# A one-layer decoder step on eight cores: values before keys in the mixer, convolution and sample work between attention steps, gate before up, and a new order of the first loads

## The reference

```
def decoder_layer(x, p, s0, conv0, ng, ...):
    h = x + 0.5 * rms_norm(swiglu(rms_norm(x, ng[0]), f1_gate, f1_up, f1_down), ng[1])
    mix, s_new, conv_new = token_mixer(rms_norm(h, ng[2]), s0, conv0, ...)
    h = h + rms_norm(mix, ng[3])
    h = h + 0.5 * rms_norm(swiglu(rms_norm(h, ng[4]), f2_gate, f2_up, f2_down), ng[5])
    gate = jax.nn.sigmoid(rms_norm(h, ng[6]) @ w_ple_gate)
    h = h + rms_norm((p @ w_ple_proj) * gate, ng[7])
    return h, s_new, conv_new
...
def token_mixer(u, s0, conv0, ...):
    q, k, v, g, r, cb, cc, ch = jnp.split(u @ w_in, points, axis=-1)
    log_a = log_sigmoid(r @ w_gate_up + b_gate) / 16
    o, s_new = gla_chunked(q, k, v, log_a, s0)
    o = rms_norm(o, gla_norm_g) * silu(g)
    oc = cb * conv3(cc * ch)
    return concat([o, oc]) @ w_out, s_new, conv_new
```

## Time and profile before

| | |
|---|---|
| median of 3 runs | 1643.7 us (1640.93 to 1648.77) |
| profiled execution | 1645.65 us, span of its slowest core 1644.0 us |
| spans of the eight cores | 1631.0 to 1644.0 us, mean granted TensorE clock 0.967 to 0.975 |
| busy, share of the span | PE 93%, DVE 44%, ACT 45%, POOL 16% |
| DMA | 305.39 MB, mean 186 GB/s |

### The profile page before, as it was taken

One profiled execution on the slowest core, in us unless ns is written; L12 is line 12 of the kernel. 1 busy time (PEld: TensorE's weight loads), 2 busy tenths in 40 slices (PEclk: granted clock), 3 DMA queues, 4 the chain that ended last, 5 costly groups with the idle time before them and its releaser, 6 DMA issues.

```text
span 1644.0 us, 27962 instructions; the slowest of 8 cores (1631.0 to 1644.0 us)
## 1 busy us (share of the span) xinstructions
PE 1537.0 (93%) x9454; PEld 1492.4 (91%) x9454; DVE 715.9 (44%) x1421; ACT 736.5 (45%) x1437; POOL 268.5 (16%) x512
## 2 busy tenths in 40 slices
PE   6999999899998999999989999799998998999996
PEld 5999889889997999989989999799998997889995
DVE  3331464543324643155554422573315754433136
ACT  3112665642147611275574124841138474511266
POOL 3211210112121221111112112022111110111110
PEclk9999999999998999998999999899999995999998
DMA  9865843468666796565446668399556443566661
GB/s 282 255 186 160 233 142 102 112 181 250 186 193 191 208 328 209 170 184 167 102 156 208 200 176 249 112 279 319 177 160 202 137 142 100 158 177 175 203 190 69
DMA packets 83452, 305.39 MB, mean 186 GB/s; under 512 B 9538, under 2 KB 12498, under 8 KB 82548
## 3 DMA queue, kind: packets, MB, share of 16 engines
q0 software_dynamic: 73040, 283.97, 58.4%
q1 hardware_dynamic: 10276, 19.65, 3.7%
HBM read 292.83 MB, written 10.75 MB: 185 GB/s over the span
## 4 chain that ended last, share of the span: by engine, by line
PE 79%; DMA 7%; ACT 6%; DVE 4%; issue 4%; DVEq 0%; SPq 0%; ACTq 0%; POOLq 0%; POOL 0%
PE ps_bank L472 78%; DMA sb_wring<-f2a 3%; DMA sb_wring<-f2b 2%; ACT L519 2%; DMA sb_wring<-f1b 1%; ACT sb_xnB L519 1%; DVE sb_hB L522 1%; DVE sb_xnB L522 1%; DMA sb_ngl<-ngl 1%; ACT sb_ta L519 1%; PE ps_bank L496 1%; ACT sb_WA L519 1%; PE ps_bank L504 0%; ACT sb_sqB L519 0%; DVE sb_WA L527 0%
## 5 line engine op out<-in xcount | busy, mean ns | idle before, releaser
L472 PE MATMUL ps_bank<-sb_xnA,sb_wring 128*128 128x344 f32 x2208 | 410.6, 332 | 19.0 <-DVE sb_WA L527 8.6
L472 PE MATMUL ps_bank<-sb_xnB,sb_wring 128*128 128x344 f32 x2208 | 396.6, 323 | 6.6 <-ACT sb_xnB L519 5.7
L472 PEld LDWEIGHTS ps_bank<-sb_xnA,sb_wring 128*128 128x128 f32 x2208 | 370.1, 197 | 27.2 <-issue 26.0
L472 PEld LDWEIGHTS ps_bank<-sb_xnB,sb_wring 128*128 128x128 f32 x2208 | 358.2, 190 | 13.5 <-issue 13.1
L472 PE MATMUL ps_bank<-sb_WA,sb_wring 128*128 128x344 f32 x1872 | 330.7, 323 | 11.4 <-DVE sb_WA L527 4.7
L472 PE MATMUL ps_bank<-sb_WB,sb_wring 128*128 128x344 f32 (+1 forms) x1904 | 333.7, 320 | 1.7 <-DVE sb_wring L522 1.0
L472 PEld LDWEIGHTS ps_bank<-sb_WA,sb_wring 128*128 128x128 f32 x1872 | 301.6, 189 | 17.8 <-issue 17.5
L472 PEld LDWEIGHTS ps_bank<-sb_WB,sb_wring 128*128 128x128 f32 x1904 | 309.1, 190 | 2.6 <-issue 2.4
L607 POOL DMA_DIRECT2D sb_wring<-f2a x132 | 69.7, 528 | 367.1 <-PE ps_bank L472 334.9
L519 ACT ACT_TABLE_LOAD x91 | 116.8, 1283 | 27.4 <-DMA sb_ngl<-ngl 14.4
L607 POOL DMA_DIRECT2D sb_wring<-f1a x132 | 69.7, 535 | 290.7 <-PE ps_bank L472 280.7
(11 more groups left out here) (198 smaller groups left out, 1647.6 us busy)
## 6 DMA issues: line engine op xcount, KB each, us to landing
sb_wring<-f1a POOLq DMA_DIRECT2D x132, 512.0 KB, 10.0
sb_wring<-f2a POOLq DMA_DIRECT2D x132, 512.0 KB, 5.5
sb_wring<-f1b POOLq DMA_DIRECT2D x48, 704.0 KB, 5.5
sb_wring<-f2b POOLq DMA_DIRECT2D x48, 704.0 KB, 5.3
sb_wring<-wca POOLq DMA_DIRECT2D x24, 512.0 KB, 6.8
sb_wring<-wo POOLq DMA_DIRECT2D x24, 512.0 KB, 5.6
sb_wring<-wpg POOLq DMA_DIRECT2D x24, 512.0 KB, 7.3
sb_wring<-wg POOLq DMA_DIRECT2D x12, 512.0 KB, 6.7
```

The source lines that it names most:

```text
L472: ins = e.matmul(out.ap, a.ap, b.ap, start=(first and i == 0), stop=(last and i == n_ - 1))
```

## The change

1. **First loads.** After `ngl` and A's x are put among the pending operations, all pending ones are issued at once; B's x follows. In the planner's model a load by SP of over 400 columns now takes link time.
2. **Gate first.** In both feed-forwards the gate product and its weights go ahead of the up product, and the gate's VectorE and ScalarE operations are queued before the up product is asked for.
3. **Mixer.** Values ahead of keys and queries, right behind E and Einv; convolution chunk 1 is no longer ahead of the keys. In tiles 0 to 3 the three attention steps now hold chunks 1, 2 and 3; in tiles 4 and 5 chunks 1 to 3 run before the steps. The weights' order in the ring follows. `Einv` moves to W from 6n (the later place of convolution chunks 2 and 3), `sp` to `S.sq`.
4. **Sample pieces.** One piece (`FIRST`) before the attention steps of tile 5, up to six (`EACH`) between `step_a` and `step_c` of each step, what is left after them; `kept` moves to `S.xn`. The wait on `gla_done` comes after the first piece.
5. **Sum of the next x.** The eight blocks of squares are added in pairs on VectorE (three adds of 688 columns per tile), and two matmuls at the end of `ple` replace the eight; the bank is held only there.
6. **Priority.** Every Exp with scale -0.5 (the second half of each 1/sqrt, after a Ln) gets 20 us of priority in the planner.
7. Helpers `sqr` and `scl` choose an engine; as called, all operations stay on the engines they had. A pending operation can have several `ways` to run; no call of the kernel gives a second one.

```diff
+FIRST = 1
+EACH = 6
+PAIR = 20.0
...
+            elif writes and ndma == 1 and width > 400:
+                self.link = max(self.link, start + 2.0) + 0.0018 * width
+                self.done[tok] = self.link + 0.5
...
-        o["Einv"] = 16 * n
+        o["Einv"] = 6 * n
...
+            keep = P.prio
+            if func == AF.Exp and scale == -0.5:
+                P.prio += PAIR
...
             for j in range(NJ):
-                o += [(fA_d[f], j, 1024, 2048), (fA_d[f], j, 0, 1024)]
+                o += halves(fA_d[f], j)
...
             o = halves(wg_d, 0) + halves(wg_d, 1)
-            for c in range(2):
-                o += halves(wca_d, c) + [(wcb_d, c, 0, 1024)]
+            o += halves(wca_d, 0) + [(wcb_d, 0, 0, 1024)]
+            o += [(wv_d, 0, 0, 2048), (wv_d, 1, 0, 2048)]
             o += halves(wkq_d, 0) + halves(wkq_d, 1)
-            o += [(wv_d, 0, 0, 2048), (wv_d, 1, 0, 2048)]
-            for c in range(2, 4):
+            for c in range(1, 4):
                 o += halves(wca_d, c) + [(wcb_d, c, 0, 1024)]
...
-                bu_ = yield from prod(S, n, fA_d[f], j, 1024)
                 bg_ = yield from prod(S, n, fA_d[f], j, 0)
...
+                later(gate)
+                bu_ = yield from prod(S, n, fA_d[f], j, 1024)
...
-                later(gate)
                 later(gated)
...
                 act(wv_(S, T, "E", pp * n, (pp + 1) * n), bk.v(0, n), AF.Exp)
-            yield from conv_chunk(S, T, 1)
+            for h2 in range(2):
+                w = yield from get(S, wv_d, h2)
...
-            done_c = 4 if last_pass else 2
+            done_c = 4 if last_pass else 1
...
             if ns:
-                go = True
-                for _ in range(2 * NS):
-                    if go:
-                        go = yield from piece()
-            prev = None
+                for _ in range(FIRST):
+                    go = yield from piece()
+            while T.idx > 0 and not gla_done[T.idx - 1]:
+                yield None
             for s in range(nch):
-                lo, hi = T.chunks[s]
-                yield pe([wv_(S, T, "kt", 0, 2 * n), wv_(S, T, "qtz", 0, 4 * n)])
-                am = step_a(s)
+                yield from prep(s)
                 if prev is not None:
                     step_d(*prev)
                 if done_c < 4:
                     yield from conv_chunk(S, T, done_c)
                     done_c += 1
-                yield pe([am.v(0, 512), W.v(o["kz"], o["kz"] + 512), Sr[gk["k"] % 2].v(0, 256)])
-                bo, oq = step_c(s, am)
+                for _ in range(EACH):
+                    if go:
+                        go = yield from piece()
+                kb, k0 = kz_at(s)
+                yield pe([ams[s], kb.v(k0, k0 + 512), Sr[gk["k"] % 2].v(0, 256)])
+                bo, oq = step_c(s, ams[s])
                 prev = (s, bo, oq)
+            while go:
+                go = yield from piece()
...
             def xprep(c):
                 xr = S.W.v((10 + c) * n, (11 + c) * n)
-                q = S.W.v((18 + c % 4) * n, (19 + c % 4) * n, r=True)
-                act(q, xr, AF.Square)
-                ts(S.W.v((10 + c) * n, (11 + c) * n, r=True), xr, gvec(0, c), None, ALU.mult, None)
-                xq.append(q)
+                k = 18 + c if c < 2 else 20 + c % 2
+                sqr(S.W.v(k * n, (k + 1) * n, r=True), xr)
+                scl(S.W.v((10 + c) * n, (11 + c) * n, r=True), xr, gvec(0, c), "dve")
+                if c % 2 and c > 1:
+                    acc = S.W.v(18 * n, 20 * n)
+                    tt(S.W.v(18 * n, 20 * n, r=True), acc, S.W.v(20 * n, 22 * n), ALU.add)
...
             yield pe(xq, [bx.v(0, n)], True)
-            xsum(0)
+            mm(bx.v(0, n), [(csr.v(C_OD, C_OD + 128, r=True), q) for q in xq])
...
             load_h(streams[0], tiles[0], c)
+        P.settle(list(P.pending))
```

More of the change, by code:

```diff
@@ L165, in op @@
             return self.emit_op(eng, fn, reads, writes, **kw)
-        new = Op(eng, fn, reads, writes, kw, self.prio)
+        ways = [(eng, fn, kw)]
+        if "other" in kw:
+            ways = [(eng, fn, {"dur": kw.get("dur")}), kw["other"]]
+        new = Op(ways, reads, writes, self.prio)
         for o in self.pending:
@@ L182, in emit_pending @@
             a.before.discard(o)
-        self.emit_op(o.eng, o.fn, o.reads, o.writes, **o.kw)
+        eng, fn, kw = o.ways[way]
+        self.emit_op(eng, fn, o.reads, o.writes, **kw)
     def pick(self):
@@ L190, in pick @@
             if o.due is None:
[L191 to L197 removed]
+                o.due = [self.ready(w[0], o.reads, o.writes) for w in o.ways]
+            for way, (eng, fn, kw) in enumerate(o.ways):
+                due, free = o.due[way], self.free[eng]
+                t = max(due, free)
+                tab = kw.get("table")
+                turn = SWITCH if tab is not None and tab != self.table else 0.0
+                late = max(0.0, t - min(max(d, self.free[w[0]]) for d, w in zip(o.due, o.ways)))
+                key = (t + turn if due > free + 0.15 else free, due - o.prio + turn + late)
+                if best is None or key < best[0]:
+                    best = (key, t, o, way)
         return best
```

132 lines of the change are left out of this document (69 added, 63 removed).

## The result

The changed kernel takes 1622.4 us (median of 4 runs, 1618.8 to 1696.3) beside 1646.2 for the kernel before on the same chip. The slowest run of each four (1696.3 and 1671.5) is in the chip's slower state, and the ratio, 0.985 [0.981, 0.990], leaves such runs out. The forecast was 1619, the range 1598 to 1640. The total came out; its terms did not, and the experiments were made to find out why. The profiled execution, 1618.8 us with a span of 1617.3, stands in the place of 1645.65 and 1644.0.

The account below looks back on a forecast made before the run. PE, 93% busy, was taken as the bound, with gains only where its stretches hold fewer products. Terms 4 + 8 + 2 + 3 + 7.5 = 24.5 off 1645.65 give 1621.1; less 2.0, 1619 us, range 1598 to 1640.

Parts of the forecast that it names:

- First loads: Kernel start: ngl and A's x go first, so PE's run without holes begins earlier; 4 us, bounds -1 to 8.
- near 22: Kernel start, a sign of being right: PE's run without holes begins near 22 us, against 26.02 before.
- the transfer of all pieces by 16.8 us at 282 GB/s: Kernel start: A's and B's x, weights and small loads up to B's last piece take 16.8 us from 2.9 us.
- This term's rival: Kernel start: shared engines bring B's x as late as A's did, weights behind it; -1 instead of 4, total 1624; chance 0.12.
- Sum of x: Ple stages of four tiles: fewer matmuls and a freed bank, less VectorE adds; 8 us, bounds -3.5 to 20.
- some 2 come back: Ple: of the slow clock's time (13 and 10 us at half clock), some 2 us are won back.
- Priority and gate first: Exp right after Ln, and feed-forward gate product before up product: 2 us together, bounds -2 to 5.
- Mixers of tiles 0 to 3: Attention's third step gets convolution chunk 3 as cover, removing one 3.00 us wait; net 3 us, bounds -8 to 10.
- Last mixer: Tile 5's attention steps interleaved with sample pieces, each hiding the other's latencies; 7.5 us, bounds 0 to 16.
- under 36 us in place of 42: Last mixer, a sign of being right: time from the samples' first store to the end of B's steps.
- Waits only change places: Rival: ple waits end on ScalarE, last mixer stays at half clock, f2a waits take the rest; about 1639; chance 0.18.
- Values no longer cover the queries: Slower rival: uncovered gap from last query product to step_a, 6.4 us in each of six tiles; 1657; chance 0.06.

Follow-up runs that it names:

- e6: Changed kernel, but at the start the third weight piece waits for only the first half of B's x: 1630.4 us, ratio 0.985.
- e2: Changed kernel with the Exp's priority set to 0: 1626.8 us, ratio 0.986.
- e14: Changed kernel, but each feed-forward block holds the gate product's PSUM bank until the block's last operation: 1628.9 us, ratio 0.987.
- e4: Changed kernel with keys and queries ahead of values again in all tiles, weights' order too: 1618.8 us, ratio 0.981.
- e10: Changed kernel with keys and queries ahead of values, and all 18 sample pieces in a row before the attention steps: 1614.6 us, ratio 0.978.
- e1: Kernel before with only the next x's squares summed on VectorE and the bank held only at the end of ple: 1628.2 us, ratio 0.987.
- e8: Changed kernel, but in tiles 0 to 3 convolution chunk 1 runs between values and keys, leaving the third attention step without one: 1625.0 us, ratio 0.985.

## Why the prediction was right in sum and wrong in its terms

The sum came out by luck: two terms were sized too small and two too large, and these errors cancelled.

**First loads: 4 forecast, 0.8 measured.** With the new order the start took 41.2 to 44.2 us in ten traces (without e6), with the old one 42.0 to 43.7 in three: nothing that can be told. The timeline of the changed kernel:

```profile
1.06 0.38 SPq L475 DMA_DIRECT2D sb_ngl<-ngl  x1
1.50 1.83 SPq L475 DMA_DIRECT2D sb_hA<-x  x4
...
10.02 0.63 PE L485 MATMUL ps_bank<-sb_xnA,sb_wring 128*128 128x344 f32 x1 [2.17 <-DMA sb_wring<-f1a]
...
14.37 0.62 PE L485 MATMUL ps_bank<-sb_xnA,sb_wring 128*128 128x344 f32 x1 [3.72 <-DMA sb_wring<-f1a]
...
19.32 6.87 POOL L635 DMA_DIRECT2D sb_wring<-f1a  x13 [16.04 <-DMA sb_hB<-x]
...
25.31 1.49 PE L485 MATMUL ps_bank<-sb_xnA,sb_wring 128*128 128x344 f32 x8 [0.73 <-DMA sb_wring<-f1a]
```

The mark "`ngl` first on SP" came true, the run without holes "near 22" did not: 25.3 against 26.02. The step that failed is the transfer of all pieces by 16.8 us at 282 GB/s. The transfers ran at 196 GB/s over the first 10 us and at 241 over the next 10. The third weight piece, which waits for B's x, could go out only at 19.32 and landed 5.9 us later; PE's run began as it came, at 25.31. The first two weight pieces, for which PE now waits 2.17 and 3.72 us, came no later (by their issue and time to landing at 9.8 and 14.2 us, 11.7 and 14.1 before): PE waits for them because A's x is there sooner. The wait of the third piece did the rest. It ended at 12.84 before and at 19.32 now, and by then hardly anything else was out, so that the transfers nearly stopped: over the four microseconds from 18 on they ran at 189, 21, 0 and 258 GB/s. Ending the wait a microsecond earlier (e6) didn't help, since the plan changed with it.

The Trainium skill, "Trainium Kernel Development and Optimization", section Key Constraints, says that the queues share 16 engines and interleave. The trace agrees: POOL's second weight piece, issued at 2.7 us, landed at 14.2, amid the x that SP had issued. This term's rival, given 0.12, was nearer: the weights behind B's x came late, and 0.8 us were left of 4.

**Sum of x: 8 forecast, 14.5 measured in ple.** Of the terms, the waits (4 net of the adds; 4.6 less idle time) and the adds (0.871 us; the new ones take 0.869) were right, and so was the place: the sum alone gives 10 to 11 us there. The step that failed is "some 2 come back" from the clock: up to 7.8 did. It could have been seen: all of a stretch's half-clock time stood in the earlier trace rows as something the denser run could win. The Trainium skill, "Perfetto Trace Analysis", section Matmul Optimizations, says that TensorE's power follows its use, so that back-to-back matmuls matter; here the stretch's clock went from 0.94 to 0.98 with less idle time before its matmuls.

**Priority and gate first: 2 forecast.** The priority can't be told from nothing in the whole; without it one stretch takes some 5 us more (e2). Gate first was costed by the 3.3 us that PE waits for such blocks; alone it wins 15 us, none of it in the feed-forwards. The step that failed asked what waits for this block, and not what this block keeps from others: bank time 7.8 us against 4.1, and the order that follows. How much of the 15 is the banks is not shown; holding 6.6 us again gave back 5.4 to 6.6 us (e14). The same page and section of the Trainium skill asks for all eight banks to be at work; in this case e14 shows what a longer hold costs in ple, 4 to 5 us.

**Mixers of tiles 0 to 3: 3 forecast, 13.1 measured on the slowest cores, 6.7 by the medians.** The size came from one wait of 3.00 us, taken for a hole between steps that a convolution chunk would cover. That reading failed: the wait ended on the last operation of such a chunk (295.20), and in the changed kernel the like waits are 4.5 and 4.4 us. What the slowest core won back was 4.5 us of idle time and 5.1 of fillers, which no list of waits shows. The cause named, the third step's cover, is one of several: taken out of the changed kernel it costs 4.8 us (5.9 by the medians), but gate first alone gives 12.6 (7.0) without it, and the sum alone 12.2 (7.5, all of it in tiles 2 and 3). With the rest of the change in place, up first costs 3.9 (2.6), and keys first 6.3 on the slowest core but 0.9 by the medians. Several routes reach the same 180 to 183 us; which of them made the gain in the changed kernel stays open.

**Last mixer: 7.5 forecast, −2.0 measured on the slowest cores, 0.9 by the medians: no gain that can be told.** The step that failed is "interleaved, the steps' latencies lie under sample pieces and the reverse". The mark, under 36 us in place of 42 from the first store to the end of B's steps, is missed (51.7 to the state's store against 44.0), and samples in a row are as fast (50.9). The granted clock of the stretch rose from 0.71 to 0.76, and no time came of it. Why two chains of one stream don't cover each other was not tried further. With keys ahead of values, so that B's values run beside A's steps, the stretch takes 63 us (e4, e10); that it is this cover which makes it is read from the order in e10's timeline and not tested by itself.

**The rivals.** "Waits only change places" is refuted by ple and mixers. "Values no longer cover the queries", the slower case, named the query writes ahead of `step_a` in all six tiles. No such wait of more than 0.7 us is in the changed kernel's list. B's two long new waits stand at `step_c` and end on the convolution, though with keys first the longest on such an operation is 2.0 us (e4). Only in the last mixer did the order of values cost, 6.9 us by e4 (4.5 by the medians). So the sum of 24.5 met the 26.7 by +13.1 and +14.5 where 3 and 8 stood, and 0.8 and −2.0 where 4 and 7.5 did.

## What to carry to other kernels

Where a build-time planner draws the order of two streams, the gain of an edit does not stay at its place and gains do not add: take each part alone and out, and compare stage by stage between equal counts of work. A list of waits understates a hole that fillers or a low clock cover: add the fillers' time and half of the time at half clock to the idle time before sizing a term. One core of one execution is one draw: look at the same stretch on all cores before a cause is named. When a shared pool of banks is tight, ask of every operation how long it keeps a bank, not only who waits for it.

## What was not expected of the hardware

The clock in ple did not follow the idle time of the stretch: it was 0.94 with 8.7 us idle and 2 fillers (kernel before, tiles 0 and 1), 0.98 with 8.9 us and 2 fillers (e1, tiles 2 and 3), and 1.00 with 8.3 us and 31 fillers (e14), which was still 1 to 3 us longer than the changed kernel. What decides it, no run varied alone. The start of one and the same code differed by 3 us between kernels (41.2 to 44.2) and by up to 4.9 us between the cores of one execution (39.9 to 44.8, e8), as much as the order of the first loads was hoped to win.
